# Block boundaries, gate sums and bias tables of a two-block transformer kernel rearranged

## The reference, cut to what matters

```
for l in range(2):                                   # first block
    mod = silu(c) @ w_ada[l] + b_ada[l]              # 3 * 1024 columns
    shift, scale, gate = split(mod)
    h = rms_norm(x, g_pre[l]) * (1 + scale) + shift
    (cq, ckv, kr, za, qb, kb, vb, zb, qc, kc, vc, zc, gcols) = split(h @ w_in[l])
    o_a = (mla(cq, ckv, kr) * silu(za)) @ w_o_mla[l]        # 8 heads
    o_b = (window attention(qb, kb, vb) + bias * silu(zb)) @ w_o_swa[l]
    o_c = (differential attention(qc, kc, vc) * silu(zc)) @ w_o_diff[l]
    y = (g0 * o_a + g1 * o_b + g2 * o_c) @ w_out[l]         # g = sigmoid(gcols)
    x = x + gate * rms_norm(y, g_post[l])
# second block: the same modulation for x and for 256 context tokens, neighbourhood
# attention with a bias table, a gated scan in both directions, w_out_2, a gated update of x,
# then a router that gives each of 16 experts its 32 best tokens, and the experts
# (gate, up and down weights of 1024 x 2752 each), a norm and the last gated update
```

## Time and profile before

| | |
|---|---|
| three runs | 2466.63, 2467.01, 2467.95 us, median 2467.01 |
| profiled execution | 2463.6 us, its span 2461.8 |
| PE busy | 1876.5 us (76%) |
| DVE, ACT, POOL busy | 494.0, 287.1, 48.2 us |
| moved | 714.92 MB, mean 290 GB/s |
| PE clock over the span | 0.871 of full |

### The profile page before, as it was taken

One profiled execution on the slowest core, in us unless ns is written; L12 is line 12 of the kernel. 1 busy time (PEld: TensorE's weight loads), 2 busy tenths in 40 slices (PEclk: granted clock), 3 DMA queues, 4 the chain that ended last, 5 costly groups with the idle time before them and its releaser, 6 DMA issues.

```text
span 2461.8 us, 25423 instructions
## 1 busy us (share of the span) xinstructions
PE 1876.5 (76%) x10518; PEld 1043.6 (42%) x10518; DVE 494.0 (20%) x1068; ACT 287.1 (12%) x703; POOL 48.2 (2%) x80
## 2 busy tenths in 40 slices
PE   5899999699999699986666666666666666666665
PEld 1668776567787568653322222122222222222211
DVE  1224322224322326743200001000000000100001
ACT  1113220112220102321000000000000000000000
POOL 0000000000000300010000000000000000000000
PEclk9899999899999899998778868887788787878787
DMA  9633554234455522257699999999999999999996
GB/s 315 189 132 116 206 193 144 73 109 159 175 195 171 176 75 76 69 210 288 248 423 422 421 422 423 422 422 422 423 423 422 422 422 423 422 422 422 423 424 272
DMA packets 149551, 714.92 MB, mean 290 GB/s; under 512 B 11711, under 2 KB 16191, under 8 KB 95904
## 3 DMA queue, kind: packets, MB, share of 16 engines
q1 hardware_dynamic: 143776, 697.08, 70.6%
q0 software_dynamic: 2016, 7.21, 1.2%
q10 hardware_dynamic: 3640, 8.94, 1.1%
HBM read 709.38 MB, written 3.80 MB: 290 GB/s over the span
## 4 chain that ended last, share of the span: by engine, by line
issue 65%; PE 28%; DVE 3%; DMA 2%; ACT 1%; POOL 0%; ACTq 0%; POOLq 0%; DVEq 0%
PE banks L757 10%; PE banks L1539 4%; PE banks L1548 3%; PE banks L762 1%; PE banks L811 1%; PE banks L1581 1%; PE banks L877 1%; DMA arena<-in_w_mods_dram 1%; PE banks L820 1%; DVE arena L2051 1%; PE banks L716 1%; PE banks L905 1%; PE banks L887 1%; DVE arena L1977 1%; PE banks L1509 0%
## 5 line engine op out<-in xcount | busy, mean ns | idle before, releaser
L2269 PE MATMUL banks<-arena 128*32 128x512 f32 (+2 forms) x3072 | 471.5, 743 | 303.9 <-DMA arena<-in_w_up_dram 298.0
L2269 PEld LDWEIGHTS banks<-arena 128*32 128x32 f32 x3072 | 128.5, 137 | 587.0 <-issue 580.4
L757 PE MATMUL banks<-arena 128*128 128x256 f32 x1536 | 344.8, 382 | 1.4 <-DVE arena L1254 1.4
L757 PEld LDWEIGHTS banks<-arena 128*128 128x128 f32 x1536 | 288.6, 191 | 43.7 <-DVE arena L1254 3.2
L2296 PE MATMUL banks<-arena 128*32 128x512 f32 x1280 | 214.3, 808 | 112.6 <-DMA arena<-in_w_down_dram 75.5
L2408 DVE SCALAR_TENSOR_TENSOR arena<-arena,banks 64x512 f32<-64x512 f32 (+1 forms) x48 | 30.5, 635 | 787.6 <-ACT arena L2321 786.9
L2296 PEld LDWEIGHTS banks<-arena 128*32 128x32 f32 x1280 | 46.7, 132 | 260.5 <-issue 259.1
L2321 ACT ACTIVATE arena<-banks 64x512 f32<-64x512 f32 (+1 forms) x48 | 26.7, 556 | 837.2 <-PE banks L2269 831.4
L1539 PE MATMUL banks<-arena 128*128 128x256 f32 x512 | 113.4, 379 | 0.2 <-DVE arena L1912 0.2
L1539 PEld LDWEIGHTS banks<-arena 128*128 128x128 f32 x512 | 96.0, 190 | 13.1 <-DVE arena L1912 0.4
L2415 DVE COPY arena<-banks 128x512 f32<-128x512 f32 x16 | 11.1, 692 | 369.6 <-PE banks L2304 369.6
(11 more groups left out here) (319 smaller groups left out, 1624.2 us busy)
## 6 DMA issues: line engine op xcount, KB each, us to landing
arena<-in_w_gate_dram SPq DMA_DIRECT2D x128, 1376.0 KB, 30.2
arena<-in_w_up_dram SPq DMA_DIRECT2D x128, 1376.0 KB, 32.1
arena<-in_w_down_dram SPq DMA_DIRECT2D x160, 1024.0 KB, 30.4
arena<-in_w_in_dram SPq DMA_DIRECT2D x68, 1024.0 KB, 7.2
arena<-in_w_mods_dram SPq DMA_DIRECT2D x48, 1024.0 KB, 7.2
arena<-in_w_out_dram SPq DMA_DIRECT2D x12, 1024.0 KB, 5.0
arena<-in_w_down_dram SPq DMA_DIRECT2D x16, 512.0 KB, 22.0
arena<-in_w_o_swa_dram SPq DMA_DIRECT2D x4, 1024.0 KB, 10.4
```

The source lines that it names most:

```text
L757: mm = pe.matmul(b[:, i * S:i * S + S], w, rhs[:, kt, :], start=kt == 0, stop=kt == 7)
L2269: mm = pe.matmul(bank[pc][32 * g:32 * g + 32, 0:w_], xsT[:, kt, CAP * e4:CAP * e4 + CAP], (wg if g < 2 else wu)[:, c:c + w_], start=kt == ...
```

## The change

- The loop over layers is unrolled.
- **Gate sums.** The gate third of the modulation no longer goes through TensorE. Its weights (`mods_now`, four loads of the same layer, right behind qb) are multiplied by the condition and summed by VectorE in `mrow` (`gate_rows`, two halves of eight instructions), and one product with a matrix of ones per 512 columns (`gate`) sums over the partitions and spreads the row. These two jobs stand in the middle of the layer. `ada` and `modT` are four each instead of six. The same in block 2 (`OWN_GATE` behind kn, `LAST_GATE` in the scan).
- **Prologue.** Eight modulation loads instead of twelve. The bias tables are laid as four row groups of 32 and multiplied side by side into four banks, half of them after `FIRST_MODS`, half after `qb` of layer 0; their DMAs are issued by GpSimd after the first `ada` job. x is squared and normalised during the modulation. The table `na_rows` is written by ScalarE's queue after qb.
- **Boundary.** `wout` in the order token half, column half; squares straight from the bank; each token half is normalised, scaled and added, and the norm of the next layer made, by itself. `xT` by token half. `AB` and the layer vectors are made before wout.
- **Block 2.** Context load, norm and columns, and the constants, are moved to the end of layer 1; the order is cT, tkc, xT2, tk, nv, gate2, rk, nv, tq, rq, with kn and vn loaded before qn.
- **End.** Each result tile is squared when it is made, and the store goes in quarters.

```diff
@@ loads and jobs
     chunk("w_in", D, COL["qb"], 512)
+    for r in (0, 512):
+        for c in (4, 5):
+            loads.append(("mods_now", r, 4, 512 * c, 512))
     chunk("w_in", D, COL["kb"], 256)
...
-        chunk("w_mods", D, 512 * c, 512)
+        if c < 4:
+            chunk("mods_next", D, 512 * c, 512)
...
-    for c in range(3):
-        jobs.append(("gate", c, ()))
...
+             ("q", 2, uq), ("q", 3, uq), ("gate", 0, ()), ("qc", 1, qc), ("rotq", 1, ()), ("kn", 0, ukv), ("kn", 1, ukv),
+             ("gate", 1, ()), ("kc", 0, kc), ("rotq", 2, ()), ("kn", 2, ukv), ("kn", 3, ukv), ("kc", 1, kc), ("rotq", 3, ()), ("v", 0, ukv), ("vc", 0, vc),
...
+    for t in range(2):
+        jobs += [("wout", 2 * t + c, (i + 2 * c, i + 2 * c + 1)) for c in range(2)]
...
-FIRST_MODS = [("ada", 0), ("ada", 1), ("modT", 0), ("ada", 2), ("modT", 1), ("ada", 3), ("modT", 2), ("ada", 4),
-              ("modT", 3), ("ada", 5), ("modT", 4), ("modT", 5)]
+FIRST_MODS = [("ada", 0), ("ada", 1), ("modT", 0), ("ada", 2), ("modT", 1), ("ada", 3), ("modT", 2), ("modT", 3)]
-MOD_LOADS = 12
+MOD_LOADS = 8
...
-ORDER2 = ("qn", "kn", "vn", "qh", "zf", "zb", "gh", "ih")
-MODS_AFTER = {"ih": (0, 1, 2, 3, 4, 5)}
+ORDER2 = ("kn", "vn", "qn", "qh", "zf", "zb", "gh", "ih")
+MODS_AFTER = {"ih": (0, 1, 2, 3)}
...
-             (("modT2", 2), ("mod", 4), ("modT2", 3), ("mod", 5)), (("modT2", 4), ("modT2", 5)))
+             (("modT2", 2), ("modT2", 3)), (("gate3", 0), ("gate3", 1)))
...
+    jobs += [("tkc", n, i["kn"]) for n in range(2)]
+    jobs += [("xT2", n, ()) for n in range(4)]
+    jobs += [("tk", n, i["kn"]) for n in range(2)]
+    jobs += [("nv", n, i["vn"]) for n in range(2)] + [("gate2", n, ()) for n in range(2)]
+    jobs += [("rk", n, ()) for n in range(2)] + [("nv", n, i["vn"]) for n in (2, 3)]
+    jobs += [("tq", n, i["qn"]) for n in range(2)] + [("rq", n, ()) for n in range(2)]
@@ the sums on VectorE, in whole
+        def gate_rows(dve, loads, half, turns, cond, acc):
+
+            both = [i for i, n in sorted(loads.items()) if n == half]
+            for i in both:
+                dve.wait_ge(ring_full[(MOD_LOADS + i) % RING], 16 * (turns + (MOD_LOADS + i) // RING + 1))
+            for k in range(4):
+                for c, i in enumerate(both):
+                    a, w = acc[:, 512 * c:512 * c + 512], ring[:, (MOD_LOADS + i) % RING, 512 * k:512 * k + 512]
+                    kt = 4 * (half - 1) + k
+                    if kt == 0:
+                        ins = nc.vector.tensor_scalar(a, w, cav[:, kt, cond:cond + 1], None, ALU.mult)
+                    else:
+                        if kt == 4:
+                            dve.wait_ge(gate_read.sem, gate_read.at(0, gate_read.n - 1 + c))
+                        else:
+                            dve.wait_ge(gate_own.sem, gate_own.at(0, gate_own.n - 1 + (c if kt in (3, 7) else 0)))
+                        ins = nc.vector.scalar_tensor_tensor(a, w, cav[:, kt, cond:cond + 1], a, ALU.mult, ALU.add)
+                    if kt == 7:
+                        ins.then_inc(gate_sum.sem, gate_sum.up())
+                    elif kt == 3:
+                        ins.then_inc(gate_read.sem, gate_read.up())
+                    else:
+                        ins.then_inc(gate_own.sem, gate_own.up())
@@ SyncE: what a slot waits for
+                    if i - RING in GATE_LOADS:
+                        half_read = gate_read if GATE_LOADS[i - RING] == 1 else gate_sum
+                        sp.wait_ge(half_read.sem, half_read.at(l, 2))
+                    elif i >= RING:
+                        sp.wait_ge(job_done.sem, made(l, LAST_USER[i - RING]))
@@ TensorE
+            def bias_tables(half):
+
+                for g in range(4):
+                    r = slice(32 * g, 32 * g + 32)
+                    pe.matmul((*SB, TB, OB)[g][0:120, :], TAB[r, 12:132], NAH[r, 512 * half:512 * half + 512],
+                              start=True, stop=True).then_inc(pro_pe.sem, pro_pe.up())
...
+            pe.wait_ge(tables_in, 160)
+            pe.matmul(MB[0:12, :], TAB[0:33, 0:12], T5[0:33, :], start=True, stop=True).then_inc(pro_pe.sem, pro_pe.up())
+            bias_tables(0)
...
+                        pe.wait_ge(gate_sum.sem, gate_sum.at(l, n + 1))
+                        mm = pe.matmul(b, C("ones"), mrow[:, 512 * n:512 * n + 512], start=True, stop=True)
...
+                if l == 0:
+                    pe.wait_ge(pro_v.sem, pro_v.at(0, 5))
+                    bias_tables(1)
@@ GpSimd
+            pool.wait_ge(const_in, 32)
+            pool.wait_ge(job_done.sem, made(0, -PRE))
+            pool.dma_start(TAB[0:33, 0:12], A["t5_tab"]).then_inc(tables_in, 16)
+            pool.dma_start(T5[0:33, :], A["t5_hot"]).then_inc(tables_in, 16)
+            for g in range(4):
+                pool.dma_start(TAB[32 * g:32 * g + 32, 12:132], A["na_tab"]).then_inc(tables_in, 16)
+                pool.dma_start(NAH[32 * g:32 * g + 32, :], A["na_hot"][:, 1024 * g:1024 * g + 1024]).then_inc(tables_in, 16)
@@ ScalarE, end of a layer
+                    act.wait_ge(cx_in, 16)
+                    for t in range(2):
+                        nc.scalar.activation(cxs[:, D * t:D * t + D], cxv[:, t, :], ACT.Square, accum_out=css[:, t:t + 1]).then_inc(cxq.sem, cxq.up())
+                for t in range(2):
+                    for c in range(2):
+                        n = 2 * t + c
+                        j = JOB_OF["wout", n]
+                        act.wait_ge(job_done.sem, made(l, j))
+                        nc.scalar.activation(E[:, 512 * n:512 * n + 512] if n < 3 else th[:, 0:512], bank[j % BANKS], ACT.Square,
+                                             scale=0.5, accum_out=s4[:, n:n + 1]).then_inc(ysq.sem, ysq.up())
+                    act.wait_ge(xup.sem, xup.at(l, t + 1))
+                    nc.scalar.activation(xnv[:, t, :], xv[:, t, :], ACT.Square, accum_out=xss[:, t:t + 1]).then_inc(xsq.sem, xsq.up())
@@ VectorE, end of a layer
                 for t in range(2):
+                    dve.wait_ge(ysq.sem, ysq.at(l, 2 * t + 2))
+                    nc.vector.tensor_tensor(ss[:, t:t + 1], s4[:, 2 * t:2 * t + 1], s4[:, 2 * t + 1:2 * t + 2], ALU.add).then_inc(v_own.sem, v_own.up())
...
+                    dve.wait_ge(yrs.sem, yrs.at(l, t + 1))
+                    js = [JOB_OF["wout", 2 * t + c] for c in range(2)]
+                    for c, j in enumerate(js):
+                        a = slice(512 * c, 512 * c + 512)
+                        nc.vector.scalar_tensor_tensor(xnv[:, t, a], bank[j % BANKS], rs[:, t:t + 1], G1[:, a],
+                                                       ALU.mult, ALU.mult).then_inc(reader(j), 1)
...
+                    nc.vector.tensor_tensor(xv[:, t, :], xv[:, t, :], xnv[:, t, :], ALU.add).then_inc(xup.sem, xup.up())
+                    x_mean(l + 1, t)
+                    x_scale(l + 1, t)
```

659 lines of the change are left out of this document (345 added, 314 removed).

## The result

The changed kernel took 2435.19 us (median of four runs, 2430.06 to 2441.22) against 2466.82 for the kernel before: ratio 0.9875, 95% interval 0.985 to 0.990. It is faster by 31.6 us. I had forecast 2418 with a range of 2406 to 2432: the direction was right, 17 us of the gain did not come. Two executions of the experiments, 3474 us of own_buffers and 2675 us of control_again, fell into a slower state that the ratios leave out, and with or without them the medians are the same to 0.2 us.

The account below looks back on a forecast made before the run. Head bound by DMAs, layers by TensorE, expert stage constant behind the router. Terms -30.8 -1.4 -11.4 -2.8 -0.5 -2.3 = -49.2 off span 2461.8 give 2412.6; plus 5.2 from span to median, 2417.8 us, range 2406 to 2432.

Parts of the forecast that it names:

- Head: Start to first projection: bound by DMA bytes; loads land at 35, then 10.4 us in series, projection at 45.4; -30.8 us.
- Boundary: Last wout product to next layer's first projection: work by token half cuts 23.6 us by 11.4 (bounds -9, -13).
- Inside the layers: Each layer: jobs removed -5.1, gate products +2.0, ring wait before kb +2.4; -0.7 per layer.
- Entry of block 2: From wout end to first attention score: 100.0 against 102.8 us, with +4.8 wait before nv; -2.8 (bounds -8, +4).
- rival (b): Ring waits: kb 7.0 twice, vn 8.1, with low clock behind each +5; +17 us, 2435; chance 0.11.
- Sums on VectorE: Gate sums: some 5.5 us a half, nothing on the path in layers; in the scan, scan 3 +1.5 us.
- rival (d): VectorE's sums cost as much as the 3.35 us reciprocal per instruction: +79 us, 2497; chance 0.03.
- Gate3: In the scan stage: gate3 leaves the path from oT to wo2; -2.5 us.
- End: After the experts: squares per tile under the last scatter, stores in quarters; -2.3 us (bounds -1, -4).
- rival (e): Expert stage: its own start, not the router, sets the stream, which hides the gain; 2467 us; chance 0.02.
- the low clock: TensorE after the kb and vn waits: up to 1.8 us more each, 5 in all; 0.4 charged, gaps being short.

Follow-up runs that it names:

- own_buffers: Changed kernel with the weights of kb, vb and block 2's nv loaded into idle memory instead of the ring; 2421.88 us, ratio 0.9817.
- control_again: Changed kernel unedited, run once more in a later group; 2431.99 us, ratio 0.9869.
- control: Changed kernel unedited, run beside the first group of experiments; 2435.41 us, ratio 0.9873.
- head_bytes: Changed kernel with two more 1 MB loads, which nobody needs, ahead of the modulation loads; 2443.04 us, ratio 0.9908.
- warm_half: Changed kernel with matmuls whose results nobody reads put in TensorE's waits, 7 of them ahead of layer 1; 2425.96 us, ratio 0.9847.
- best: own_scan with matmuls whose results nobody reads in TensorE's remaining waits; 2398.73 us, ratio 0.9737.
- own_scan: Changed kernel with the edits of own_buffers and scan_order together; 2411.83 us, ratio 0.9781.
- thin_layers: Changed kernel with gate sums on 8 of 512 columns everywhere but in the scan, leaving out work; 2433.45 us, ratio 0.9877.
- scan_order: Changed kernel with scan-stage loads and sums reordered and gate3 behind the last state products; 2427.62 us, ratio 0.9844.
- thin_sums: Changed kernel with gate sums on 8 of 512 columns in the scan alone, leaving out work; 2427.95 us, ratio 0.9841.
- own_scan_again: The kernel own_scan unedited, run once more beside best on the same chip; 2415.16 us, ratio 0.9789.

## Why the prediction was right, and where it failed

**Head (-30.8, came -32.6).** The step was right: bytes, not the tables, set it. The tail in series held in its sum (its first term should be 1.6 by the 6.34 of 32 passes that it names, not 1.4; 1.93 came): the last modulation product began at 33.20 and the projection 10.4 us later. That it fits is partly luck. The eight passes took 1.93 at the lower clock, in control 1.07, and there the projection follows after 9.1; this is also why the starts in the table fall into 42.0 to 42.4 and 43.4 to 43.7. The loads were there 1.8 us sooner than the 35 that I took, since they flow at 350 to 394 GB/s; head_bytes has some 383 for added ones.

**Boundary (-11.4, came -12.6).** Right in its parts (those behind the last product add up to 7.65, where 7.8 is written), and 11.0 us long in every run without filling. Of the difference 1 us is the lower clock that I had charged here: it was paid in layer 1, and more than once.

**Inside the layers (-0.7 each, came +3.2 and +2.8).** The gain was real: the two `ada` and `modT` jobs left the ticks, and from the first score of layer 1 to the first wo product before took 184.7 us and after 179.4, -5.4 where -5.1 was summed. The two gate products cost 2.2 (I had 2.0; four passes at the 0.605 that I named would be 2.4). What was mis-sized is the price of a wait. I charged the wait for kb, +2.4, and it was 3.0. I did not charge the slow stretches of layer 1: 1.4 on the first projection (1 of it stood in the boundary's sum), 1.7 on `qb`. From the first projection of layer 1 to its first score that is +8.0 instead of +4.4. In layer 0 the slow stretch behind the wait for kb costs 1.6, the second set of table products 1.1 (I had taken it to fill half of the wait for kb, which was 2.82 all the same) and a wait for qc 0.6; the first projection was 1.7 slower and `qb` 1.7 faster than before, which cancels. own_buffers takes the wait before kb away and gets layer 1 to 355.3, below before's 356.8, with a fast `qb`; that the wait costs its 3 us is shown by experiment, the 355.3 is partly a lucky clock.

**Entry of block 2 (-2.8, came +1.6).** `nv` needs both of its loads in its first product, and I priced one (that the second makes the difference is not shown): 5.61 of wait came where 4.8 was summed, and behind it 3.0 us at the lower clock, where I had 0.4. `tkc` cost 2.9 for the clock, where I had 1.7. The two stood in my rival (b), with their chance of 0.11, as one case in which all ring waits are long at once. own_buffers gives back 8.5 here, warm_half 5 to 6. (The terms of this sum add up to 100.3, not to the 100.0 written.)

**Attention (0, came +1.5).** I had no term for it. All of it is the slow start of the first scores, behind the 3.56 us of rotations that now stand right before them. In warm_half and best, which fill this wait, the stretch is back at before's 153.5; so it is in own_scan, which has the wait unfilled and yet no slow start.

**Sums on VectorE.** 0.68 us an instruction, as taken from the earlier trace rows, so rival (d) is out. Under the projections they cost nothing (thin_layers). In the scan they cost 6 us against a scan with thin ones. Against before's distances they cost 1.9 and 0.6, where I had 1.4 and 0.1; 1.0 of the difference is a wait for their own load. What I missed was the other column: taking the `mod` products out would have let the last scan follow after 7.45 us, a gain of 4 that I had not counted and that the sums ate.

**Gate3 (-2.5, came +0).** It did leave the path from oT to wo2: 5.2 us before, 2.8 after. But I did not ask what is queued behind it where it now stands. There it waits for scan 3 to free a bank, and the last state products wait for it, +2.3; and TensorE, idle for 9.9 of the 16 us before it, begins wo2 at half the clock, +3.1. scan_order takes the first away, warm_half the second.

**End (-2.3, came -3.2)** and the expert stage of constant length (1252.3 us from the first expert product to the last scatter in both) were right, so every us at the router was one at the end, and rival (e) falls. In the experiments it is constant to 3 us only: from the first expert product to the end 1264.6 to 1267.6, longest in thin_sums, scan_order and own_scan_again.

Summed up: in the profiled execution 15.7 us of the forecast gain are missing, and 3.9 more came at the head, the boundary and the end than forecast, so 19.6 are to be explained. The lower clock holds 13.5 of them: kb of layer 0 1.6, first projection of layer 1 1.4, its `qb` 1.7, `tkc` 1.2 and `nv` 2.6 above what I had charged, first attention products 1.5, `mod` products of the first scan 0.4, wo2 3.1. (1.0 of the 1.4 was charged at the boundary, where it is in the 3.9 that came in excess; net of it the clock holds 12.5.) Gate3 ahead of the state products has 1.8 above the 0.5 that I had for it, the sums in the scan 1.0. The 3.3 left are the waits for kb, nv and qc that were longer than priced, and the table products of layer 0. In medians the miss is 17.4, because the profiled execution was the fastest of its four: the median lies 6.9 above the span, where I had taken 5.2.

The failed step is thus the low clock. Behind the new waits for kb and nv, which the prediction put at "up to 1.8 more, 5 in all; I have 0.4, since these gaps are short", it cost 4.7: 1.6, 0.1 and 3.0. And it cost 10.9 at the other gaps (the first projection and `qb` of layer 1, `tkc`, the first scores, the first `mod` products of the scan, wo2), of which the prediction had charged 2.7. That the clock and not the loads or operands makes them slow is shown by warm_half and best, which change neither and have `tkc`, `nv`, the first scores and wo2 at full speed (best has no wait before `nv`, warm_half had it and filled it). That the result has the number of rival (b), 2435, is by half chance: its clock was right (5 behind these waits), its longer waits did not come (7.0 at each kb and 8.1 at nv, where 3.0 and 5.6 came), and the losses in the scan and at wo2 were in no rival.

The Trainium skill (TensorE: Matmul & The Clock Gate, "The HAM clock gate") calls the cost of the ramp under 1% of a typical span. The 16.4 us between own_scan_again and best, in which the 2.8 of the expert stage are still contained, are 0.7%, so that agrees. They are also half of all that this change gained.

What stays open: when exactly the clock falls. `qb` of layer 1 was slow in after and in best, and that of layer 0 in before, fast in own_buffers and control_again, behind the same 1.8 us wait or a shorter one.

## What to carry to other kernels

Price a wait of TensorE as the wait plus a slow restart: here gaps of 1.7 to 6 us cost up to another 3.1 us on the products behind them, on top of themselves, and some cost nothing (0.1 behind the wait for kb of layer 1, 1.6 behind that of layer 0). When a long wait is cut into several short ones the sum of the gaps can fall while the restarts multiply: ahead of the first expert product the trace of before has 8 stretches at the lower clock, that of after 13. So look at the granted clock of each stretch before and after.

When a load is put into a ring, ask which load it pushes back and how soon that one is needed; the loads of kb, vb and nv, moved to idle memory, were worth 13.5 us. And when work is moved from one engine to another, look for what the freed engine could have done with the room before giving the room away.
